# A depthwise convolution's steps in another order, and in other gaps of VectorE's program

## The reference, cut to what matters

```python
def conformer_mixer(u_glu, hist, w_dw, b_dw, ln_g, ln_b):
    glu = u_glu[..., :CONV_CH] * jax.nn.sigmoid(u_glu[..., CONV_CH:])
    xh = jnp.concatenate([hist.astype(glu.dtype), glu], axis=1)
    c = causal_depthwise(xh, w_dw) + b_dw.astype(glu.dtype)
    c = layernorm(c, ln_g, ln_b)
    return jax.nn.silu(c), xh[:, -(CONV_WIDTH - 1):]
...
    t_inv = lax.linalg.triangular_solve(eye + lower, jnp.broadcast_to(eye, lower.shape),
                                        left_side=True, lower=True, unit_diagonal=True)
    u = t_inv @ v_beta
    w = t_inv @ (k_beta * jnp.exp(gc)[..., None])
...
    mixed = jnp.concatenate([conv_out, o.reshape(n, t, GDN_V).astype(x.dtype)], axis=-1) @ p['w_out']
```

## Time and profile before

| what | value |
|---|---|
| median of three runs | 1319.46 us (1318.15 to 1323.41) |
| the profiled execution's own time | 1324.24 us |
| its span, first to last instruction | 1322.3 us |
| PE busy | 1265.9 us, 96% |
| DVE busy | 441.3 us, 33% |
| DMA | 470.14 MB, 356 GB/s over the span |
| mean granted TensorE clock | 0.990 of full |

### The profile page before, as it was taken

One profiled execution on the slowest core, in us unless ns is written; L12 is line 12 of the kernel. 1 busy time (PEld: TensorE's weight loads), 2 busy tenths in 40 slices (PEclk: granted clock), 3 DMA queues, 4 the chain that ended last, 5 costly groups with the idle time before them and its releaser, 6 DMA issues.

```text
span 1322.3 us, 17194 instructions
## 1 busy us (share of the span) xinstructions
PE 1265.9 (96%) x6486; PEld 599.7 (45%) x6486; DVE 441.3 (33%) x1263; ACT 216.5 (16%) x452; POOL 28.9 (2%) x74
## 2 busy tenths in 40 slices
PE   9999998999999999999999999999999999999997
PEld 5879764786663333333333333333333333333332
DVE  3665966245232332223322223322222233222222
ACT  2341222322130111001110011101000110010012
POOL 4000010010000000000000000000000000000000
PEclk8999998999999999999999999999999999999999
DMA  9421426497979999999999999999999999999993
GB/s 312 148 96 33 151 92 216 178 344 312 409 290 416 395 428 428 427 427 428 429 428 428 429 429 428 428 428 428 429 429 428 429 429 428 428 429 428 428 427 123
DMA packets 56821, 470.14 MB, mean 356 GB/s; under 512 B 6884, under 2 KB 7109, under 8 KB 32061
## 3 DMA queue, kind: packets, MB, share of 16 engines
q1 hardware_dynamic: 51146, 458.94, 83.7%
q0 software_dynamic: 2816, 9.80, 1.9%
q10 hardware_dynamic: 2819, 0.83, 0.3%
HBM read 463.84 MB, written 6.29 MB: 356 GB/s over the span
## 4 chain that ended last, share of the span: by engine, by line
PE 67%; DMA 27%; DVE 4%; ACT 1%; issue 1%; SPq 0%; DVEq 0%; ACTq 0%
PE bank L1042 35%; DMA ring<-in_w_gu 26%; PE bank L591 13%; PE bank L1092 3%; PE bank L861 3%; PE bank L1074 2%; PE bank L1056 2%; DVE region_p L1747 2%; PE bank L747 1%; PE bank L1068 1%; PE bank L755 1%; PE bank L667 1%; DMA ring<-in_cache_mem_v 1%; PE bank L940 1%; DMA region_m<-in_x_prompt 1%
## 5 line engine op out<-in xcount | busy, mean ns | idle before, releaser
L1042 PE MATMUL bank<-ring,region_p 128*64 128x512 f32 x2304 | 509.6, 594 | 22.4 <-DMA ring<-in_w_gu 22.2
L1042 PEld LDWEIGHTS bank<-ring,region_p 128*64 128x64 f32 x2304 | 161.5, 137 | 354.3 <-issue 298.6
L2058 DVE TENSOR_SCALAR region_p<-bank 128x512 f32<-128x512 f32 x32 | 22.1, 692 | 655.3 <-PE bank L1074 655.3
L1042 PE MATMUL bank<-region_m,region_p 128*64 128x512 f32 x752 | 168.6, 595 | 7.7 <-DMA region_m<-in_w_gu 7.7
L591 PE MATMUL bank<-hT,ring 128*128 128x264 f32 x512 | 121.4, 394 | 0.0
L591 PEld LDWEIGHTS bank<-hT,ring 128*128 128x128 f32 x512 | 97.4, 194 | 16.7 <-issue 0.4
L1042 PEld LDWEIGHTS bank<-region_m,region_p 128*64 128x64 f32 x752 | 52.3, 137 | 115.8 <-issue 96.5
L1496 ACT COPY region_p<-bank 128x264 f32<-128x264 f32 x33 | 12.5, 379 | 510.7 <-PE bank L1068 510.7
L2032 DVE TENSOR_TENSOR xT<-xT,bank 128x264 f32<-128x264 f32 x248 | 89.4, 422 | 19.1 <-PE bank L1092 19.1
L1092 PE MATMUL bank<-region_p 64*128 64x264 f32 x496 | 72.0, 409 | 0.0
L1042 PE MATMUL bank<-region_p 128*64 128x512 f32 (+1 forms) x260 | 63.0, 605 | 0.3 <-DVE region_p L2017 0.3
(11 more groups left out here) (385 smaller groups left out, 891.8 us busy)
## 6 DMA issues: line engine op xcount, KB each, us to landing
ring<-in_w_gu SPq DMA_DIRECT2D x96, 2048.0 KB, 30.0
ring<-in_w_dn SPq DMA_DIRECT2D x48, 2048.0 KB, 35.3
region_m<-in_w_gu SPq DMA_DIRECT2D x31, 2048.0 KB, 29.9
region_m<-in_w_dn SPq DMA_DIRECT2D x16, 2048.0 KB, 35.3
ring<-in_w_in SPq DMA_DIRECT2D x6, 2048.0 KB, 15.8
ring<-in_cache_mem_k SPq DMA_DIRECT2D x7, 1024.0 KB, 15.9
ring<-in_cache_mem_v SPq DMA_DIRECT2D x6, 1024.0 KB, 9.7
ring<-in_w_mk SPq DMA_DIRECT2D x2, 2048.0 KB, 7.8
```

The source lines that it names most:

```text
L1042: ins = pe.matmul(bank[n][u * SLOTS:(u + 1) * SLOTS, :], lhs, rhs, start=start, stop=stop)
L2058: dve.tensor_scalar(xg, bank[0][:, :], 7.0, None, ALU.min).then_inc(sem("glu_clipped"), 1)
```

## The change

The list of steps gets a new order, and the numbers of steps at the places change; three places are new. Block 0 runs its first fifteen steps alone, since block 1's input comes one level later. Then block 1 and block 0 alternate until block 0 is done, block 2 and block 1, block 3 and block 2; the last fifteen steps are block 3's alone. Places of the 140 steps, before and after, in the order of the program: after `k_pad` 0 and 9; level 2 after `inv_d` 0 and 6, after `inv_t` 10 and 10; level 3, 7 and 7, then 10 and 10; level 4, 7 and 7, then 13 and 13; level 5, 7 and 2, then 13 and 15; after the samples' output 0 and 5; after `v_blocks` 6 and 6; after `o_rows(1)` 8 and 17; the rest, behind the outer products, 59 and 33.

```diff
--- before.py
+++ after.py
@@ -1731,7 +1731,19 @@
 
 
 
-            conv_steps = [(f, j) for pair in ((0, 1), (2, 3)) for j in range(TAPS + 4) for f in pair]
+
+
+            def conv_order(lead, steps):
+                at = [lead] + [0] * CF
+                yield from ((0, j) for j in range(lead))
+                for f in range(CF):
+                    while at[f] < steps:
+                        for g in (f + 1, f):
+                            if g < CF:
+                                yield g, at[g]
+                                at[g] += 1
+
+            conv_steps = list(conv_order(15, TAPS + 4))
             conv_mark = [chain[0]] * CF
 
             def conv_some(n):
@@ -1782,6 +1794,7 @@
                         ins = dve.tensor_copy(k_pad[:, :, 4 * m:4 * m + 4],
                                               qkv[:, H:2 * H, TP + 4 * m:TP + 4 * m + 4].rearrange("p h j -> p j h"))
                     ins.then_inc(sem("k_pad"), 1)
+                    conv_some(9)
                 elif key[0] == "v_tok":
                     c = key[1]
                     wait_filled(dve, *key)
@@ -1800,14 +1813,14 @@
                     wait_filled(dve, *key)
                     drained(dve.tensor_copy(inv_t[c].rearrange("p h n -> p (h n)"), ps(key)[:, :]), key)
                     if c == 1 and lv >= 2:
-                        conv_some({2: 10, 3: 10, 4: 13, 5: 13}[lv])
+                        conv_some({2: 10, 3: 10, 4: 13, 5: 15}[lv])
                 elif key[0] == "inv_d":
                     lv, c = key[1:]
                     wait_filled(dve, *key)
                     drained(dve.copy_predicated(inv_u[c], masks[:, lv, :].bitcast(U32).unsqueeze(1).to_broadcast(
                         [P, H, P]), by_head(key)), key)
-                    if c == 1 and 3 <= lv < LEVELS - 1:
-                        conv_some(7)
+                    if c == 1 and 2 <= lv < LEVELS - 1:
+                        conv_some({2: 6, 3: 7, 4: 7, 5: 2}[lv])
                 elif key[0] == "s_kq":
                     wait_filled(dve, "s_kq")
                     drained(dve.tensor_copy(s_kq[:, :], ps(("s_kq",))[:, 0:BH]), ("s_kq",))
@@ -1834,6 +1847,7 @@
             dve.wait_ge(sem("s_vn"), 1)
             drained(dve.tensor_tensor(mix[:, H:2 * H, TP:T], s_o.rearrange("p (b h) -> p h b", b=TS),
                                       s_kq.rearrange("p (b h) -> p h b", b=TS), ALU.add), ("s_rd",))
+            conv_some(5)
 
             def o_rows(c):
                 wait_filled(dve, "o_t", c)
@@ -1854,7 +1868,7 @@
                                                op0=ALU.mult, op1=ALU.add)
             drained(ins, ("state", 1))
             o_rows(1)
-            conv_some(8)
+            conv_some(17)
             for b in range(NG):
                 wait_filled(dve, "s_outer", b)
                 m, j = divmod(b, 4)
```

## The result

The changed kernel takes 1314.38 us in the median of 18 runs (1309.52 to 1319.06), the kernel before 1322.43 us in 18 runs beside it (1317.86 to 1324.34). The ratio is 0.9949, with a 95% interval of 0.9937 to 0.996: faster by about 0.5%, some 7 us, where 10 us were forecast. (The two medians are 8.0 us apart and the two means 7.5 us; the ratio on record stands for 6.7 us, and the text goes by it.) The median of the changed kernel lies within the stated range, but its distance from the kernel before is a third smaller than my sum had it. The kernel before itself is at 1322.43 us in these 18 runs and was at 1319.46 us in the three that the forecast started from.

What follows compares the result with a forecast made beforehand. PE's idle time behind the convolution's taps, and the low clock after it, was taken as the price. -0.1 + 1.9 + 1.6 - 0.5 + 3.8 + 3.2 gave near 10.0 us: 1319.5 to 1309.5 us, range 1306.5 to 1315.5 us.

Steps and rivals of the forecast that it cites:

- 1.9 - 0.1 - 0.5 + 3.8 = 5.1 us: PE's waits: 1.9 won at level 5's copies, 0.1 lost at level 2, 0.5 ahead of `w_neg`, 3.8 won ahead of `ln_mean`.
- the lone tap's 0.52 us: On DVE, a tap that waits for its own predecessor starts 0.52 us behind it, against 0.396 us for interleaved taps.
- the drains that come late: Level 5: fifteen steps behind the copies end at 164.25 us, the last `inv_d` drains were due at 162.7 us; 0.5 us given back.
- The upper bound of 0.66 us for a lone step: On DVE, a lone tap costs at most 0.66 us, if its wait costs as much as one for another engine.
- The 0.1 us at level 2: Six lone steps behind `inv_d` of level 2 take 3.00 us in 2.83 us of idle time; cost 0.1 us.
- that it reaches the end: Loads wait for PE and move with it, so the gain at `w_out` counts in full at the end.
- So I expect the clock to stay high: another 1.63 us: Last level's `inv_x`: with 0.3 us of idle time left, its sixteen products take 2.02 instead of 3.65 us.
- the 3.2 us at `ln_mean`: Without PE's gap ahead of `ln_mean`, full clock saves 2.11 us there and 1.11 us at `mv` 0.
- 4.85 us: Slow products behind PE's two waits, 1.63 + 2.11 + 1.11 us, all booked as gain from the clock.
- a sign of being wrong: Granted clock under 1 between 158 and 225 us; others: lone taps over 0.55 us apart, a grown DMA wait before the experts.
- The rival that came nearest: Clock stays low at `inv_x`, `ln_mean` or both though the waits go: gain 6.8 or 5.7 us, chance 0.15.
- The estimate beside it: If the slow products' 4.85 us needn't all be there in other executions, the whole gain lies between 5.7 and 10 us.

Runs made afterwards that it cites:

- r7: Changed kernel with PE kept busy in the two waits for the last sample values, by two and three products, which was too long: 0.9949 of before.
- s2: Changed kernel with PE kept busy by one added call in each of the two waits for the last sample values: 0.9927 of before.
- r1_before: Kernel before, run again unchanged: ratio 0.9994; its profile has a mean clock of 0.996.
- r3: Kernel before with two taps instead of seven ahead of the copies of level 5, nothing else changed: 0.9997 of before.
- s1: Kernel before with PE kept busy by two added calls ahead of the last `inv_x` and four ahead of `ln_mean`: 0.998 of before.
- r4: Changed kernel with ten instead of fifteen steps behind the copies of level 5, five more in the rest: 0.9936 of before.
- s3: Changed kernel with ten instead of fifteen steps behind the copies of level 5, the same kernel as r4 run again: 0.9932 of before.
- r5: Changed kernel with level 5 as before, seven and thirteen steps, and 30 in the rest: 0.9965 of before.
- r6: Kernel before with PE kept busy by four added products ahead of the last `inv_x` and seven ahead of `ln_mean`, too long: 1.0007 of before.
- p2_after: Second further profile of the changed kernel, unchanged: low clock of 3.4 us behind `w_neg`, none at the sample values, mean clock 0.997.
- s4: Changed kernel with ten steps behind the copies of level 5 and one busy call in each wait for the last sample values: 0.9925 of before.

## Why the prediction was wrong

**Right: what the waits are worth.** The sum had 1.9 - 0.1 - 0.5 + 3.8 = 5.1 us for them, and at one clock the kernels are 5.4 us apart; PE's own rows give 5.09 us, and the other 0.3 us have no row. Each of its steps is in the profile: the lone tap's 0.52 us, the wait that is left ahead of `inv_x`, the drains that come late and PE's wait ahead of `w_neg`, the 0.9 us left ahead of the outer products, the 4.8 us of slack at the end. (The upper bound of 0.66 us for a lone step doesn't follow from its rows, 0.48 + 0.14 is 0.62 us; with 0.52 us measured nothing hangs on it.) The 0.1 us at level 2 wasn't lost: from one `inv_x` to the next it's 12.17 us in both.

**Right: that it reaches the end.** From the first expert product on both kernels take the same time, 938.3 and 938.5 us. The loads follow PE.

**Wrong: the clock.** The step that failed is "So I expect the clock to stay high: another 1.63 us" together with the 3.2 us at `ln_mean`. What it says of its own places is right: 3.65 us became 2.02 us, 3.89 became 1.78 us, 7.98 became 6.87 us. Together these terms are 4.85 us of the sum, and the mean clocks of the runs give 1.0 to 1.3 us. I booked the end of two low stretches as a gain of 4.85 us, and looked for new ones only among the gaps near `ln_mean`. Two came up. One is behind the wait of 0.44 us ahead of `w_neg`, which the sum itself had put there, at 0.5 us and nothing for the clock: 3.4 us of low clock followed in four of five profiles, 1.35 us in the mean (in four of seven with r7's and s2's, 1.0 us). It's what the prediction had named as a sign of being wrong, a granted clock under 1 between 158 and 225 us. The other is behind two waits that the change doesn't touch, 1.25 and 1.48 us in the first profile (1.17 to 1.43 and 1.48 us over the ten) with 1.07 us of products between them, full clock in five of five profiles before and low in four of five after: 2.05 us in the mean. By these profiles 4.85 - 1.35 - 2.05 = 1.45 us is left, and 5.1 + 1.45 = 6.6 us is near what the ratio says (0.0051 x 1320 = 6.7 us); with five profiles of each kernel that closeness is partly luck. A second fault is that the 4.85 us come from one profiled execution with a low mean clock (0.990), and were booked for all; r1_before's profile has 3.4 us instead of 6.8 us of low clock at `ln_mean`.

**The rival that came nearest** is that of the clock, which had 6.8 us (chance 0.15). It named a cause, though, that happened only in part: the clock doesn't stay low at its two places, it falls at two others, one of them behind a short gap that was left. The sentence from the Trainium skill (TensorE: Matmul & The Clock Gate, Part 1) said that the number of slow matmuls at a start differs from run to run; the profiles agree, with 0, 6.8 or 10.2 us of low clock in the first 25 us. The estimate beside it was 5.7 to 10 us, and the gain came out within that. The low stretches further on vary too: `ln_mean`'s was 3.4 or 6.8 us long.

**What is shown and what isn't.** Shown is that the waits are worth their 5.4 us and that the clock added only 1.0 to 1.3 us instead of 4.85: by 101 runs with a clock, by r3, whose `inv_x` is at full speed without any gain, and by s1, which keeps PE busy in both waits and wins 2 of 4.85 us. That low clock comes up behind `w_neg` and in the attention is in the profiles. How much each stretch costs is less sure: without the first one (r4 and s3) the clock is worth 2.6 us more, twice its 1.35 us, and without the second (r7 and s2) 1.8 us, near its 2.05 us, each give or take 0.7 or 0.8 us. That the stretch in the attention comes with the change rather than by chance is likely, with none of six profiles against four of five. Why the attention's waits are spared where the clock fell at `ln_mean`, 100 us earlier, stays open. It isn't only that fall: r5, r6 and s1 have no low clock there and pay in the attention, but the two profiles with ten steps have neither. p2_after has neither as well. And why the two remedies don't add up isn't known either; with six runs each the clocks of s2, s3 and s4 can't be told apart, and the first 25 us, whose clock varies by up to 5 us of time, are in all of them.

**A better version.** Ten steps instead of fifteen behind the copies of level 5, one number: 0.9936 and 0.9932 of before against the changed kernel's 0.9949 and 0.9954. It spends 2 us of the 4.8 us of slack at the end to take away a wait of 0.44 us. The 0.5 us of that wait are sure at one clock; the rest of its 3.2 us is clock, and the two intervals against before overlap the changed kernel's.

## What to carry to other kernels

The waits that fell away on the bottleneck engine were worth their own length, 5.1 us forecast and 5.4 us measured. That holds for the waits of the whole chain only: the five taps of level 5 by themselves moved a wait from one place to another (r3). The slow products behind a wait aren't a price of that wait alone: the low clock can come up behind the next wait instead, one as short as 0.44 us or one 100 us further on that nobody touched, so book a part of it only. Where single executions scatter, put the time against the mean granted clock of each run: work and waits show as a shift of the line, here to 0.1 us for the kernel before, whose medians lie between 1318.4 and 1322.4 us. And when idle time is filled with moved work, leave it short of full where an engine waits for what stands behind.

## What the runs showed of the hardware that was not expected

- PE's granted clock fell behind a wait of 0.44 us (0.50 us in one) ahead of `w_neg` in four of the changed kernel's five profiles and in none of r7's and s2's, and stayed full behind waits of the same 0.44 us one and two steps earlier in all of them. The products ahead of `w_neg` are narrow ones, of 8 columns (L835, 1.85 us for sixteen); whether they have to do with it wasn't tried.
- A wait of 2.20 us was followed by low clock in five of five profiles of one kernel (3.4 us) and by full clock in r5, with the same instructions of PE around it.
- The time of an execution is a straight line of its mean granted clock, 1.13 us per 0.001, over eleven kernels and 185 runs; the scatter of 2 to 3 us between runs of one kernel is nearly all clock. The largest single part of it in the profiles lies in the first 25 us: 0, 6.8 or 10.2 us of low clock over all twenty, worth up to 5 us.
